# Token mixers: late products in five whole half tiles a chunk, and D x made by ScalarE

## What is computed

```
# GLA and HGRN2 (8 heads together), per chunk
b        = cumsum(log_decay)
o_inter  = (q * exp(b)) @ state
scores_ij = sum_d q_id k_jd exp(b_id - b_jd)        # i >= j
o        = o_inter + scores @ v
state    = state * exp(b_last) + (k * exp(b_last - b))^T @ v
y        = rms_norm(o) * silu(gate)
# Mamba-2 (16 heads, 4 groups), per chunk
w        = exp(b_i - b_j) * (C B^T) * dt_j          # causal
y        = w @ x + (C @ h) * exp(b)
h        = h * exp(b_last) + (x * dt * exp(b_last - b))^T @ B
y        = rms_norm((y + D * x) * silu(z))
# and, independent of all of these until the merge
gates    = h_norm @ w_gates                         # 1024 x 1024 times 1024 x 3072
```

## Time and profile before

| | us |
|---|---|
| median of 3 runs | 2033.29 |
| lowest and highest | 2032.44, 2037.49 |
| the profiled execution | 2036.86 |
| its span in the trace | 2034.5 |
| the mixers, first and last late matmul (L1612) | 579.0 and 1081.5 |
| PE busy in the whole span | 1921.0 (94%) |
| DVE, ACT busy in the whole span | 1449.6 (71%), 1053.1 (52%) |

### The profile page before, as it was taken

How to read it: one execution, slowest core, us unless ns; L and a number is a source line. 1 busy time by engine, 2 the same in 40 slices (tenths; PEclk the granted TensorE clock), 3 DMA queues, 4 the chain that set the end, 5 groups by cost and what they waited for, 6 DMA issues and landing times. The chain is left out here.

```text
span 2034.5 us, 26573 instructions
## 1 busy us (share of the span) xinstructions
PE 1921.0 (94%) x10542; PEld 1575.9 (77%) x10543; DVE 1449.6 (71%) x1567; ACT 1053.1 (52%) x1250; POOL 218.0 (11%) x176
## 2 busy tenths in 40 slices
PE   6999999999999999999998999995999999999993
PEld 5789888888988777777776888874788888888881
DVE  5967467667326878777775656556889988999975
ACT  5224444544314545444444244323777888878763
POOL 3310000000030000000001000012122222222210
PEclk9999999999999999999998999997999999999997
DMA  5241332423255557646537644543999999999986
GB/s 168 86 145 63 125 99 98 135 94 102 95 157 151 162 152 177 169 128 149 161 118 279 217 195 192 229 170 141 350 376 385 387 385 383 392 387 385 383 343 260
DMA packets 212413, 436.08 MB, mean 214 GB/s; under 512 B 28018, under 2 KB 151042, under 8 KB 184770
## 3 DMA queue, kind: packets, MB, share of 16 engines
q1 hardware_dynamic: 179394, 355.68, 49.9%
q10 hardware_dynamic: 20864, 53.49, 7.5%
q0 software_dynamic: 12032, 25.22, 3.2%
HBM read 369.67 MB, written 81.43 MB: 222 GB/s over the span
## 5 line engine op out<-in xcount | busy, mean ns | idle before, releaser
L1612 PE MATMUL psum<-h_hi,l_hi 128*128 128x512 f32 x384 | 158.2, 412 | 3.3 <-PEq L58 3.3
L1612 PE MATMUL psum<-h_lo,l_hi 128*128 128x512 f32 x384 | 160.7, 418 | 0.0
L1612 PE MATMUL psum<-h_hi,l_lo 128*128 128x512 f32 x384 | 158.1, 412 | 0.0
L2763 DVE TENSOR_TENSOR gu_lo<-up_raw,gu_hi 128x2048 fp32r<-128x2048 f32 x64 | 146.3, 2287 | 13.2 <-ACT gu_hi L2706 13.0
L2706 ACT CAST gu_hi<-up_raw 128x2048 fp32r<-128x2048 f32 x64 | 122.2, 1912 | 34.5 <-PE u_ps L2835 34.4
L1259 ACT COPY l_out<-psum 128x512 f32<-128x512 f32 x48 | 28.2, 587 | 166.3 <-PE psum L1612 161.0
L2479 PE MATMUL mpsum<-y_hi,wb_hi 128*128 128x512 f32 x256 | 103.1, 403 | 9.8 <-DVE y_lo L2237 9.2
L2835 PE MATMUL g_ps<-gu_hi,xeT_hi 128*128 128x512 f32 x256 | 105.3, 411 | 5.9 <-DVE xeT_lo L2772 5.9
L806 DVE TENSOR_TENSOR w_lo<-w_raw,w_hi 128x512 fp32r<-128x512 f32 x90 | 61.9, 689 | 65.3 <-ACT w_hi L662 65.3
L662 ACT CAST w_hi<-w_raw 128x512 fp32r<-128x512 f32 x90 | 55.8, 622 | 91.8 <-PE ps L931 91.3
L2835 PE MATMUL g_ps<-gu_hi,xeT_lo 128*128 128x512 f32 x256 | 101.8, 398 | 0.0
(11 more groups left out here) (471 smaller groups left out, 5393.6 us busy)
## 6 DMA issues: line engine op xcount, KB each, us to landing
up_raw<-moe SPq DMA_DIRECT2D x62, 1024.0 KB, 8.0
gate_raw_a<-moe SPq DMA_DIRECT2D x33, 1024.0 KB, 8.4
gate_raw<-moe SPq DMA_DIRECT2D x33, 1024.0 KB, 8.4
dn_raw_a<-moe SPq DMA_DIRECT2D x31, 1024.0 KB, 7.3
dn_raw<-moe SPq DMA_DIRECT2D x31, 1024.0 KB, 8.0
w_raw<-w_in SPq DMA_DIRECT2D x26, 1024.0 KB, 6.0
l_raw<-w_gates ACTq DMA_DIRECT2D x24, 512.0 KB, 5.0
s_gates<-l_out ACTq DMA_DIRECT2D x48, 256.0 KB, 4.3
```

The lines of the kernel that those rows point to most:

```text
L1612: ins = nc.tensor.matmul(psum[:, bank, :], w[t % 2][:, k, :], x[:, k, half * 512:half * 512 + 512], start=i == 0, stop=i == LATE_MM - 1, s ...
L2763: nc.vector.tensor_tensor(gu_lo[p][:], gu_raw[p][:], gu_hi[p][:].bitcast(F32), ALU.subtract).then_inc(gu_ready, 1)
```

## The change

PE's 15 slots of 8 late matmuls become five runs of 24, a whole half tile each (`fill(LATE_MM)`), and the mixers' own work of a chunk stands in five groups between them: levels 1 and 2, C B^T and Mamba's state; levels 3 and 4, the transposes of B and `ssm_means`; the transposes of x and levels 5 and 6; the transposes of keys, the outputs and `inter_ps`; the state update, `intra(c, 0)`, then the diagonal and level 0 of the chunk after, `mean_a`, and `intra(c, 1)`. So `intra(c, 1)` moves into the body of its own chunk, and the diagonal and level 0 into that of the chunk before. In the last chunk the transposes of keys and the state update are left out, since nobody reads that state.

DVE follows: `factors` for levels 0 and 1 and the `dec` behind them are done at the end of the chunk before; the state of GLA and `intra_in(c, 0)` move to the next body; `gla_hgrn_out` is cut in two; the making of `wd` moves behind `scores_in(2)` and `factors(4)`, and `cbm` stands right behind it. ACT's `late(h0 - 1)` opens the body, levels 5 and 6, the copy of B's transposes and `ssm_scale` stand behind `late(h0 + 1)`, and the second group of Relu and the exponential over 128 x 2048 ahead of `late(h0 + 2)`.

`D * x` is made by ACT in place of x: `x_skip`, eight activations on 128 x 128 tiles with `d_col` as their scale, behind `late(h0 + 2)`. DVE then adds it with one instruction in place of eight.

The diff, cut to its core:

```diff
@@ ScalarE
+            def x_skip(c):
+                act.wait_ge(xT_ready, c + 1)
...
+                for k in range(8):
+                    ins = nc.scalar.activation(x_in[:, k, :], x_in[:, k, :], ACT.Copy, scale=d_col[:, k:k + 1])
+                ins.then_inc(xs_ready, 1)
...
             def body(c):
                 b, h0 = c % 2, PREFIX + PER_CHUNK * c
+                late(h0 - 1)
+                for lv in (2, 3, 4):
+                    relative(c, lv)
                 if c:
                     gla_hgrn_scale(c - 1)
...
                 late(h0)
-                relative(c, 5)
...
                 late(h0 + 1)
+                relative(c, 5)
+                relative(c, 6)
+                act.wait_ge(bT_ps_ready, c + 1)
...
+                nc.scalar.copy(flat(bT[:]), ssm_ps).then_inc(bT_ready, 1)
                 if c:
                     ssm_scale(c - 1)
-                relative(c, 6)
                 differences(range(SSM_HEADS // 2, SSM_HEADS))
+                act.wait_ge(seg_ready, SSM_HEADS * (c + 1))
+                nc.scalar.activation(wmat, wmat, ACT.Exp, scale=-1.0).then_inc(wexp_ready, 1)
...
                 late(h0 + 2)
...
+                x_skip(c)
                 late(h0 + 3)
@@ VectorE
             def x_in_sum(c):
                 dve.wait_ge(intra_used, 2 * c + 2)
-                for k in range(8):
-                    ins = stt(yt[:, k, :], x_in[:, k, :], d_col[:, k:k + 1], yt[:, k, :], ALU.mult, ALU.add)
-                ins.then_inc(xd_ready, 1)
+                dve.wait_ge(xs_ready, c + 1)
+                tt(yt[:], x_in, yt[:], ALU.add).then_inc(xd_ready, 1)
@@ TensorE
             def body(c):
                 b = c % 2
-                diagonal(c)
-                if c:
-                    intra(c - 1, 1)
-                fill(SLOT)
-                level(c, 0)
-                fill(SLOT)
+                fill(LATE_MM)
                 level(c, 1)
-                fill(SLOT)
                 level(c, 2)
...
-                fill(SLOT)
-                level(c, 3)
                 if c:
                     ssm_state(c - 1)
-                fill(SLOT)
-                if c:
-                    ssm_means(c - 1)
+                fill(LATE_MM)
+                level(c, 3)
+                level(c, 4)
                 pe.wait_ge(cbm_ready, c + 1)
...
+                if c:
+                    ssm_means(c - 1)
+                fill(LATE_MM)
...
                 level(c, 5)
-                fill(SLOT)
                 level(c, 6)
-                fill(2 * SLOT)
-                pe.wait_ge(qk_ready, NE * c + NE)
+                fill(LATE_MM)
...
                 ins.then_inc(inter_ready, 1)
-                fill(SLOT)
+                fill(LATE_MM)
...
                 intra(c, 0)
-                fill(SLOT)
-                pe.wait_ge(state_ready, c + 1)
+                if c < LAST:
+                    diagonal(c + 1)
+                    level(c + 1, 0)
+                    pe.wait_ge(state_ready, c + 1)
...
                 ins.then_inc(ms_ready, 1)
-                fill(SLOT)
+                intra(c, 1)
```

More of the change, by code:

```diff
@@ L1334, in body @@
                 late(h0 + 2)
[L1335 to L1342 removed]
+                x_skip(c)
                 late(h0 + 3)
+                if c < LAST:
+                    act.wait_ge(kT_ps_ready, c + 1)
+                    nc.scalar.copy(flat(k_in[b][:]), mid_ps[:, 0:CT * P]).then_inc(kT_ready, 1)
+                    relative(c + 1, 0)
                 act.wait_ge(o_ready, c + 1)
@@ L1348, in body @@
                 if c < LAST:
-                    relative(c + 1, 0)
                     relative(c + 1, 1)
-                late(h0 + 4)
             late_load(2)
@@ L1364, in _ @@
             relative(0, 1)
-            late(4)
             for c in range(NCH):
                 body(c)
+            late(PREFIX + PER_CHUNK * NCH - 1)
             gla_hgrn_scale(LAST)
@@ L1452, in gla_hgrn_out, with gla_hgrn_state @@
                 tt(ya, g_in[:], ya, ALU.mult).then_inc(ya_ready, 1)
+            def gla_hgrn_state(c):
+                dve.wait_ge(upd_ready, c + 1)
+                own.link(tt(state[:], state[:], b_in[c % 2][:, :, CH - 1:CH].to_broadcast([P, CT, P]), ALU.mult))
+                tt(state[:], state[:], mid_ps[:, 0:CT * P].rearrange("p (a e) -> p a e", e=P), ALU.add).then_inc(state_ready, 1)
             def ssm_state(c):
@@ L1527, in body @@
                 tt(wd[b][:, 0, :], wmat[:, :, CH - 1], tok[:, c, 0, :], ALU.subtract).then_inc(wdarg_ready, 1)
-                scores_in(2)
-                dec(i0 + 6)
-                factors(4)
-                late(h0)
                 dve.wait_ge(cb_ready, c + 1)
@@ L1534, in body @@
                     .then_inc(cbm_ready, 1)
+                dec(i0 + 6)
+                late(h0)
                 if c:
+                    gla_hgrn_out(c - 1)
                     ssm_state(c - 1)
                 scores_in(3)
+                factors(c, 5)
+                scores_in(4)
+                factors(c, 6)
                 dec(i0 + 7)
-                factors(5)
                 late(h0 + 1)
-                scores_in(4)
-                factors(6)
                 dve.wait_ge(xT_ready, c + 1)
@@ L1554, in body @@
                 tt(q_in[b][:, 2:8, :], q_in[b][:, 2:8, :], b_in[b][:], ALU.mult).then_inc(q_dec_ready, 1)
+                dec(i0 + 8)
+                late(h0 + 2)
+                if c:
+                    ssm_out(c - 1)
+                dec(i0 + 9)
+                dec(i0 + 10)
                 dve.wait_ge(wexp_ready, c + 1)
@@ L1568, in body @@
                 tt(yt[:], inter_ps.rearrange("p (k t) -> p k t", t=CH), eb_in[:], ALU.mult).then_inc(inter_used, 1)
-                late(h0 + 3)
-                dve.wait_ge(upd_ready, c + 1)
-                own.link(tt(state[:], state[:], b_in[b][:, :, CH - 1:CH].to_broadcast([P, CT, P]), ALU.mult))
-                tt(state[:], state[:], mid_ps[:, 0:CT * P].rearrange("p (a e) -> p a e", e=P), ALU.add).then_inc(state_ready, 1)
-                dve.wait_ge(inter_used, c + 1)
-                intra_in(c, 0)
+                if c < LAST:
+                    factors(c + 1, 0)
+                    dec(i0 + 11)
+                    factors(c + 1, 1)
+                    dec(i0 + 12)
             project_stored(dve)
@@ L1579, in _ @@
             late(1)
+            for lv in range(2):
+                factors(0, lv)
+                dec(lv + 3)
+            late(3)
             for c in range(NCH):
@@ L1783, in _ @@
             pe.wait_ge(const_ready, 3)
+            diagonal(0)
+            level(0, 0)
             for c in range(NCH):
                 body(c)
-            intra(LAST, 1)
             fill(LATE_MM)
```

113 lines of the change are left out of this document (52 added, 61 removed).

## The result

The changed kernel takes 2043.40 us (median of 7 executions, 2038.94 to 2048.63); the kernel before, run beside it, 2037.49 us (7, 2030.15 to 2040.02). The ratio is 1.0044 with a 95% interval of 1.0025 to 1.0063: the change makes the kernel slower by some 0.44%, 9 us, with 5 to 13 us in the interval (the medians differ by 5.9). The forecast was 2028.0, that is 5.3 us faster. With four more executions the median of before itself moved from 2033.29 to 2037.49, so part of the distance to 2043.4 is in the yardstick; the sign is not.

A forecast was written before the change was run, and what follows sets the result against it. PE was the engine to shorten, its waits set by a ring through the 1 MB load, DVE and ACT. Periods -4.2, chunk 0 -1.6, last chunk -2.7, clock +3.2 made -5.3: 2028.0 us against 2033.3, range 2017 to 2042.

The forecast's parts named there:

- run D: Fourth of PE's five runs of 24 late matmuls; forecast to wait 2.4 or 3.0 us for ACT's copy `late(h0 + 2)`.
- run C: Third of PE's five runs of 24 late matmuls; forecast to wait 1.7 us for ACT's copy `late(h0 + 1)`.
- The load: SP's 1 MB `load_bb` into `wmat`: DVE's `wd` was forecast 16.5 to 17.3 us after its issue.
- D x at nothing: DVE's eight instructions becoming one (2.2 us to 1.2), costed at nothing because DVE waits some 6 us for the big load.
- the ring: Loop through a chunk, big load to `wd`, ACT, PE's `inter_ps`, next load: forecast period 56.8 us, 0.6 us less a chunk.
- The clock: PE partly at 1.2 GHz after long waits: 1.06 us a fall, three of four long waits, +3.2 us.
- part three: New PE waits for ACT to empty the one late bank: 1.7 and 2.4 to 3.0 us a chunk, about 34 us in all.
- the clock falls at every late copy: Rival (15%): all eight chunks lose PE's clock behind the one bank, 1.06 us each, +8.5 us, so 2033.
- The ring closed: PE's return path, 12.5 us from `inter_ps` to the next load's issue; landing 29.5 us after `inter_ps`; period 56.8 us.
- Edges: First and last chunk of the mixers: chunk 0 gains 1.6 us from 8 changes fewer, the last chunk 2.7 us.
- The rival that ended slower: Rival (20%): `x_in` and `z_in`, issued in the big load's midst, delay it 2 us a period, so 2042.
- The rival that the load lands sooner: Rival (20%): the big load takes 1.3 us less than 17.3, each period is 1.3 us shorter, -9, so 2019.

## Why the prediction was wrong, point by point

**Right, by its own steps.** The chain from `wd` to the first `inter_ps` product: the forecast put run D's start at +15.3 to +15.9, then 5.80, 0.6 and the outputs ahead of `inter_ps`; the chunks at full clock have 25.7 us, and `wd` to run D in the chunk shown is 866.32 - 850.47 = 15.85. The waits: 1.7 us for run C was 1.38 in five of the seven chunks (0.33 and 1.17 in the others), "about 34 us in all" was 30.0; `cbm` had 4.2 us in all, 0.6 a chunk, though two chunks had 1.03 and 1.37; none for the squares. The load: 16.8 us in the mean from issue to `wd` (15.2 to 17.7), of a forecast 16.5 to 17.3. D x at nothing. And with the clock at full speed the ring gives 25.7 + 14.8 + 16.8 = 57.3 us a period, half a microsecond above the forecast's 56.8.

**Wrong, the clock (step "The clock").** It priced a fall at 1.06 us and took three, 3.2 us. Five of the seven chunks lost it, and by their way from `wd` to `inter_ps` beyond the 25.7 us of the others (25.0 for the last chunk, which has no transposes of keys) that cost 1.5, 2.6, 1.5, 2.7 and 1.6 us: 9.9 us, so 6.7 us too little. Both factors failed. The price was read from one stall, and only from the slot behind it. The trace of before held a dearer one, behind the 3.8 us wait of the earlier trace rows, which the forecast didn't use:

```profile
740.41 0.78 PE L1612 MATMUL psum<-h_lo,l_hi 128*128 128x512 f32 x1
...
744.11 1.50 PE L1643 MATMUL psum<-q_lv,k_lv 128*64 128x64 f32 x24
745.53 0.50 PE L1612 MATMUL psum<-h_hi,l_hi 128*128 128x512 f32 x1
```

Its slot took 744.11 - 740.41 = 3.70 us in place of 2.07 and the level behind it 1.42 in place of 0.82 (838.55 to 839.37): 2.2 us, twice my price, and near the 2.6 and 2.7 of the two dearest falls of after. The count failed already in part three. The forecast had four long waits and let three of them lose the clock: run D's wait was to be 3.0 us in the chunks where ACT casts a weight tile behind the copy for run C (2.00 us) and 2.4 in those where it issues a load in its place (1.47). But all seven waits were long. With the load to issue, ACT's next step stood 856.38 - 854.36 = 2.02 us behind the copy, with the cast 796.56 - 794.58 = 1.98:

```profile
856.38 0.56 ACT L1281 ACTIVATE ex<-ex 128x384 f32<-128x384 f32 x1 [1.46 <-issue]
```

```profile
794.58 0.56 ACT L1260 COPY l_out<-psum 128x512 f32<-128x512 f32 x1
...
796.56 0.54 ACT L1281 ACTIVATE ex<-ex 128x384 f32<-128x384 f32 x1
```

Five of seven is near the forecast's share of three in four, but by luck, for the forecast let the length of a wait decide, and the waits that lost the clock are not the longer ones. In the first two periods waits of 2.94 and 3.01 us kept the clock; the second of them, and the granted clock of the run behind it:

```profile
750.73 0.47 PE L1634 MATMUL psum<-h_hi,l_hi 128*128 128x512 f32 x1 [3.01 <-ACT l_out L1260]
```

```profile
750.73:756.50 5.77, 5.77 (x26) 4.64 (x26) 5.77 (x7) 3.41 (x9) 0.00 (x0) 1.00 0.12 45
```

And this shorter one lost it, so that its run took 7.2 us:

```profile
806.46 0.47 PE L1634 MATMUL psum<-h_hi,l_hi 128*128 128x512 f32 x1 [2.94 <-ACT l_out L1260]
```

The rival "the clock falls at every late copy" had the same mechanism, with eight falls for the five measured and the same low price: at the 2.0 us a fall that was measured it would have been 2041 instead of 2033 (-8.5 + 8 x 2.0 = +7.5).

**Wrong, the return path (step "The ring closed").** From the end of `inter_ps` to the issue of the load the forecast had 12.5 us; it is 14.8 from its first product, which by the spacing of before is 13.1 from its end. The step that was mis-sized is the means. They were taken at 1.31 us, as in the earlier trace rows where late products follow. Between level 0 and the second half of `intra` they take 1.91:

```profile
829.69 1.98 PE L1785 MATMUL psum<-y_out,mean_a 128*128 128x512 f32 x4
831.60 1.09 PE L1707 MATMUL psum<-dn_raw_a,xdt 128*64 128x128 f32 x16
```

The 1.31 was too short a reading as well: in the kernel before, the slot behind the means took 2.36 us (887.91 to 890.27) in place of 2.07, so 0.29 of what they cost stood there. The other 0.3 us come with the new neighbours; the cost of a change between kinds of products had been put on slots alone. With the load of 16.8 us this comes to 13.1 + 16.8 = 29.9, where the forecast had 29.5, that is 12.5 and 17.0 for the load. What is left is 0.5 us a period, 3.4 us in seven.

**Wrong, chunk 0 (step "Edges").** Forecast -1.6 us for eight changes fewer, measured +0.1 (the first row of the table). Two of the twelve slots ahead of `inter_ps` already stood together, so seven changes went, and the late products took 22.9 us in place of 23.9. Against this 1.0 stand 0.9 us of waits (0.78 of them at the bank, at 619) and 0.3 us more in the mixers' own steps. By the same count a full chunk loses nine changes and not ten, at 1.4 us as shown above and not 2.0. The last chunk gave 1.6 us behind `inter_ps`, where 1.7 + 0.4 = 2.1 had been forecast.

The account: -5.3 forecast; +6.7 for the clock, +3.4 for the periods at full clock, +1.7 for chunk 0 and +0.5 for the end make +7.0, where the two traces differ by 7.1.

**The rival that ended slower was wrong in its mechanism.** It had the load land later because `x_in` and `z_in` are issued in its midst. They are, 842.50 - 832.74 = 9.8 us behind it (forecast 9.5), but the load took 16.8 us in the mean, and in the kernel before, where those came 14 us behind, the chunks in which DVE waited for it took 16.6 to 19.0. That the time of 2043 lies near its 2042 is chance. **The rival that the load lands sooner** took it at 1.3 us a period; it was 0.5 us sooner than the 17.3.

**What the forecast didn't ask.** It followed the ring and said what would be late next, but it took ACT's order behind `wd` as given by the work. That was a choice: three of the exponentials, 3.3 us, feed no step of PE ahead of run D, and the copy of 0.6 us behind them is what the whole chunk waits for.

## What to carry to other kernels

When slots of work that share one bank are joined to long runs, the copy that empties the bank can come onto the critical path, as it did here: put it in the copying engine's queue ahead of all that isn't needed before that bank, and only then judge the joining (here 1.0044 became 0.9911 by that alone). Price a stall on TensorE at its own length plus what the engine does next at half clock: in five of seven chunks a long run behind a 3 us wait paid another 1.5 to 2.7 us. An order that puts a step right behind the one load it waits for, with everything else ahead of it, is cheap to try by itself and was worth 0.5%.

## What the runs showed of the hardware

Waits of nearly the same length, 2.94 to 3.02 us, lost TensorE's clock in five chunks and left it alone in two, in one and the same execution; what tells them apart stays open. Shorter waits lost it too: 1.84 us in the kernel with run D's copy early, 1.92 and 2.14 with both copies early, 1.61 with the load in two halves. One of 2.03 in the kernel before kept it. Eight products within the 3 us wait kept it in every chunk for the run behind.

A broadcast load of 0.5 MB took 15.3 us from issue to landing where one of 1 MB took 17.0: behind other loads on the queue its size told little. Issued 1.8 us sooner as a whole, the load of 1 MB was used 1.6 us sooner.

A group of four 128x512 products (`mean_a`) took 1.31 us ahead of late products, whose slot then took 0.29 us more than others, and 1.91 us between groups of 64-wide ones. So its neighbours made 0.3 us of the difference; the other 0.29 us had only been counted in the next group.
